# Modulation weights as raw stationary tiles with two columns moving, and value tiles behind the first scores

## Chip, cores and metric

One core of one Trainium2 chip runs the whole program. The metric is the device time of one execution in microseconds, from a few runs of the same kernel; beside them stands one profiled execution, on which all rows are.

## What is computed

A chain of transformer layers on 256 tokens of 1024 features, all float32. The first block has two layers with modulation: each takes a vector c (and c_ctx for the 256 context tokens) to six vectors of 1024 numbers, which scale, shift and gate its norms and its outputs. Layer 0 mixes with a differential attention and a neighbourhood attention over tokens and context, layer 1 with a grouped-query attention with sinks; each is followed by a SwiGLU network. The second block has four layers: sliding-window attention (swa), a gated linear recurrence, a latent attention (mla) and swa again, each followed by an attention over a memory of 256 tokens and by a convolutional feed-forward network. Cut to what the change touches:

```
for layer in range(2):
    mod_x = split(silu(c) @ ada_w[layer] + ada_b[layer], 6)          # ada_w: 1024 x 6144
    mod_c = split(silu(c_ctx) @ ada_w[layer] + ada_b[layer], 6)
    h_x = rmsnorm(x, g) * (1 + mod_x[1]) + mod_x[0]
    x = x + mod_x[2] * mixer(h_x, h_c)
    h_x = rmsnorm(x, g2) * (1 + mod_x[4]) + mod_x[3]
    x = x + mod_x[5] * swiglu(h_x)
```

## The kernel before

All weights come as one stream of 785 units of 128 x 1024 float32 (0.52 MB), in the order of use, into a ring of six slots (`RING`). SyncE's queue loads unit u once `unit_used` says that unit u - 6 is done (`load`, L532). A float32 product is made of three products of rounded halves: ScalarE copies a unit to `ring_high` (rounded, `feed`, L1205), GpSimd, or VectorE for the first 19 units (`early_low`, L2089), writes the rest in place as `ring_low` (`low_part`, L2393), and TensorE (PE) does high x high, high x low, low x high (`product`). The semaphores `unit_high` and `unit_ready` count the units in order; PE waits on those counts. Where nothing is rounded (scores, transposes, probabilities times values, sums by a product with `mean_of`) PE does full float32 products from the raw tiles.

The modulation weights are 96 units: 16 at the start (`ada0a`), 48 during the attention of layer 0 (`ada0b`; 8 groups of layer 0 and 4 of layer 1), 32 during that of layer 1 (`ada1`). Four units make a group of 512 modulations. `ada_products` (L689) moves the 512 columns of a weight row through PE against `cond4`, which holds the two condition vectors, each as high and low part, in its first columns: two k by two halves, four instructions a unit. The sums stand in 4 rows of a bank; ScalarE copies them to `ada_rows` (L1247), PE turns them in four small transposes (`ada_turn`, L707), ScalarE copies those to `ada_cols` (L1251), and VectorE adds the two parts and the bias into `mods` (`modulations`, L2066).

The start: PE does groups 0 to 3 and, between them, the squares of x (`squares_by_token`, L716: 8 tiles by 4 products, a 128x128 tile of squares stationary and one column of `mean_of` moving). Then `spread_both` (L727) spreads the norm's scale over a bank, VectorE scales x (`scaled_both`, L1811; after its first two instructions it does the rest of the gains and the last early low parts), and the first projection begins, `project("ab", ...)`.

Each attention is written for all engines with the same loop over steps (PE L843, ScalarE L1317, VectorE L1882): scores of later heads, row minima on VectorE, exponentials on ScalarE, transposes of the probabilities on PE, copies out of the bank, products with the values, a last transpose. Layer 0's (`at0`, 16 steps) and layer 1's (`at1`, 8 steps) go one step ahead and have modulation work in slots between their parts (`fill`, L855; the slots are written out in `ADA0` and `ADA1`, L2424); the others go two steps ahead. Their first scores wait for all queries, keys and values. The engines of a queue work in program order, so what is issued first is done first.

```
                    for e in part:
                        wait_unit(u + e)
                        for kk in range(2):
                            k = 2 * e + kk
                            w = unit(u + e, 512 * kk, 512)
                            c4 = cond4[:, 4 * k:4 * k + P]
                            one = pe.matmul(banks[b][:, :], c4, w[0], start=(k == 0), stop=False)
                            mm = pe.matmul(banks[b][:, :], c4, w[1], start=False, stop=(k == KD - 1))
                            release(one)
                        state["owed"] += 1
```

Of the kernel before, what the change touches and what calls it, by code (L numbers as in the profile page):

```python
# [8 lines left out]
P = 128  # L9
T = 256  # L10
# [12 lines left out]
N_COND = P + 4 * (KD - 1)  # L23
# [99 lines left out]
UNITS, N_UNITS = unit_bases()  # L123
COLS, N_COLS = column_layout()
# [30 lines left out]
def write_program(nc, ins, out, ledger):  # L155
# [7 lines left out]
    with ExitStack() as ctx:  # L163
# [23 lines left out]
        cond4 = sb("cond4", N_COND, fp32r)  # L187
        ada_rows = sb("ada_rows", 512)
        ada_cols = sb("ada_cols", 16)
# [335 lines left out]
        with nc.Block() as block:  # L525
# [3 lines left out]
            def _(sp):  # L529
# [51 lines left out]
            def _(pe):  # L581
# [8 lines left out]
                def wait_unit(u):  # L590
                    pe.wait_ge(unit_ready, u + 1)
# [13 lines left out]
                def wait_high(u):  # L605
                    pe.wait_ge(unit_high, u + 1)
# [11 lines left out]
                def project(st, u0, n_tiles, src, n, depth=KD, ready=None, base=0, per_unit=1, after=None):  # L618

                    width = P * per_unit  # L620
                    opened = 0
# [18 lines left out]
                    for m in range(opened, n_tiles):  # L640
# [3 lines left out]
                        b = m % 4  # L644
# [18 lines left out]
                def project_v(st, u0, n_groups, src, tok_tiles, depth=KD, width=T, units=2, after=None):  # L663


                    n = 0
                    per = depth // units
                    for j in range(n_groups):
                        u = u0 + units * j
                        for e in range(units):  # L670
                            wait_unit(u + e)
                        for t in range(tok_tiles):
                            b = n % 4
# [9 lines left out]
                            n += 1  # L683
                        state["owed"] += units
# [4 lines left out]
                def ada_products(l, g, u, part=range(4), b=7):  # L689

                    if 0 in part:
                        claim(b)
                    for e in part:
                        wait_unit(u + e)
                        for kk in range(2):
                            k = 2 * e + kk
                            w = unit(u + e, 512 * kk, 512)
                            c4 = cond4[:, 4 * k:4 * k + P]
                            one = pe.matmul(banks[b][:, :], c4, w[0], start=(k == 0), stop=False)
                            mm = pe.matmul(banks[b][:, :], c4, w[1], start=False, stop=(k == KD - 1))  # L700
                            release(one)
                        state["owed"] += 1
                    if 3 in part:
                        mm.then_inc(*mark(proj_ready, "ada", l, g))
                        reader[b] = ("ada_rows", l, g)

                def ada_turn(l, g, b=7):  # L707

                    pe.wait_ge(*when("ada_rows", l, g))
                    for t in range(4):  # L710
                        mm = pe.transpose(banks[b][:, 4 * t:4 * t + 4], ada_rows[0:4, P * t:P * (t + 1)],
                                          const("ident", P)[0:4, 0:4])
                    mm.then_inc(*mark(proj_ready, "ada_cols", l, g))
                    reader[b] = ("ada_colsread", l, g)

                def squares_by_token(st, part):  # L716

                    for k in part:
                        pe.wait_ge(*when(st, "sq", k))
                        for i in range(4):  # L720
                            mm = pe.matmul(banks[6][:, i:i + 1], sq2(k)[:, P * i:P * (i + 1)], mean_of[:, 0:1],  # L721
                                           start=(k == 0 and i == 0), stop=(k == KD - 1), skip_group_check=True)
                        if k == KD - 1:
# [119 lines left out]
                def attention(st, items, needs, ada=None):  # L843
# [11 lines left out]
                    def fill(slot):  # L855
                        if ada_fill(ada, slot):
# [3 lines left out]
                            else:  # L860
                                ada_turn(*group)

                    def scores(s, a):
# [6 lines left out]
                        if s == 0 and a == 0:  # L870
                            for ev in needs:
# [26 lines left out]
                    def values(s):  # L898
# [3 lines left out]
                        claim(b)  # L902
                        for n, (a, blocks) in enumerate(fulls(d)):
# [62 lines left out]
                def ffn(name, src, ready, aside=None):  # L966
# [13 lines left out]
                    def gate_up(r, t, halves=(0, 1)):  # L980
# [4 lines left out]
                        for half in halves:  # L985
                            u = gate_unit(t) + half
                            out = banks[4 + t % 2][:, T * half:T * (half + 1)]
                            pe.wait_ge(unit_high, r * (3 * BODY) + (u + 1))
# [1597 lines left out]
```

## Time and profile before

| | |
|---|---|
| median of 3 runs | 2815.99 us (2813.96 to 2816.88) |
| the profiled execution: its time | 2817.64 us |
| its span, first to last instruction | 2815.8 us |
| mean granted TensorE clock | 0.961 |
| PE busy | 2646.3 us (94%), 19840 instructions |
| GpSimd busy | 1819.9 us (65%) |
| ScalarE busy | 1465.3 us (52%) |
| VectorE busy | 1122.9 us (40%) |
| read from HBM | 418.52 MB, 149 GB/s over the span |

The granted clock is the share of full speed that the chip gave TensorE in a stretch; 1.00 is 2.4 GHz, 0.50 is 1.2 GHz. A matmul's busy time is longer than its distance from the next one, since they are pipelined: a price is best taken from the distance of starts. In the windows "x" counts instructions, and one float32 product in the code can be more than one. Two ways to name a line are used: that of the code, and that of a helper which several stages share (L601 to L616 are all projections, L879 all scores, L893 all transposes of probabilities, L908 all products with values).

### The profile page before, as it was taken

The page shows a single profiled execution, that of the slowest core. Times are in us where ns is not written, and L with a number is a line of the kernel's source. Part 1 is how long each engine was busy: PE and PEld are TensorE (multiplying, and loading weights), DVE is VectorE, ACT ScalarE, POOL GpSimd, SP SyncE. Part 2 cuts the span into 40 slices and gives each one's busy share as a digit, 9 for nine tenths or more (in the row PEclk, how much of TensorE's full clock was granted, in tenths as well). Part 3 has the DMA queues.
Part 4 walks back from the last instruction along what each step waited for, and adds up shares of the span by engine and source line. Part 5 has one row for each costly group of instructions (what it writes and reads, how often), then busy time and mean ns, then how long its engine had stood idle before and what let it go on. Part 6 is the DMA issues. An engine that isn't in the chain of part 4 may idle for free.

```text
span 2815.8 us, 52622 instructions
## 1 busy us (share of the span) xinstructions
PE 2646.3 (94%) x19840; PEld 2506.8 (89%) x19840; DVE 1122.9 (40%) x2642; ACT 1465.3 (52%) x2586; POOL 1819.9 (65%) x770
## 2 busy tenths in 40 slices
PE   7998889999999999999999998999989999989998
PEld 6887769999997899988899988899978899888998
DVE  5227634122155521234343365433443433463434
ACT  5326735445445544444555576555545555464655
POOL 0437647888875778772568865488645688535786
PEclk7999999999999999999999988999999999989999
DMA  6325424555543545541345543255423455323554
GB/s 226 120 82 173 149 91 166 184 180 180 185 158 126 190 160 182 179 146 65 120 157 179 183 134 130 100 188 185 149 91 120 139 182 182 125 76 113 172 180 141
DMA packets 115637, 421.75 MB, mean 150 GB/s; under 512 B 12832, under 2 KB 14112, under 8 KB 114976
## 3 DMA queue, kind: packets, MB, share of 16 engines
q1 hardware_dynamic: 115200, 417.00, 44.0%
q8 instruction: 111, 1.82, 0.3%
q10 hardware_dynamic: 288, 2.62, 0.3%
q14 instruction: 38, 0.31, 0.0%
HBM read 418.52 MB, written 1.05 MB: 149 GB/s over the span
## 4 chain that ended last, share of the span: by engine, by line
PE 50%; issue 22%; POOL 20%; DVE 4%; ACT 2%; DMA 1%; POOLq 0%; SPq 0%; DVEq 0%; ACTq 0%
POOL ring_low L2395 20%; PE bank L610 9%; PE bank L616 9%; PE bank L611 9%; PE bank L601 6%; PE bank L602 6%; PE bank L603 6%; PE bank L908 2%; PE bank L879 2%; PE bank L760 1%; ACT scr L1332 1%; PE bank L926 1%; PE bank L721 0%; PE bank L893 0%; DVE xt L2267 0%
## 5 line engine op out<-in xcount | busy, mean ns | idle before, releaser
L2395 POOL TENSOR_TENSOR ring_low<-ring,ring_high 128x1024 fp32r<-128x1024 f32 x766 | 1819.7, 2406 | 978.0 <-ACT ring_high L1210 767.3
L610 PE MATMUL bank<-high,ring_high 128*128 128x256 f32 (+1 forms) x3372 | 856.4, 290 | 3.6 <-ACT ring_high L1210 1.7
L611 PE MATMUL bank<-low,ring_high 128*128 128x256 f32 (+1 forms) x3372 | 849.5, 288 | 0.0
L610 PEld LDWEIGHTS bank<-high,ring_high 128*128 128x128 f32 x3372 | 647.1, 192 | 10.8 <-ACT ring_high L1210 4.3
L611 PEld LDWEIGHTS bank<-low,ring_high 128*128 128x128 f32 x3372 | 647.3, 192 | 6.4
L1440 ACT ACTIVATE ring_high<-ring 128x1024 fp32r<-128x1024 f32 x448 | 467.5, 1053 | 92.2 <-DMA ring<-in_units 91.7
L616 PE MATMUL bank<-high,ring_low 128*128 128x256 f32 (+1 forms) x3372 | 491.6, 288 | 0.0
L616 PEld LDWEIGHTS bank<-high,ring_low 128*128 128x128 f32 x3372 | 445.2, 192 | 5.6
L1210 ACT ACTIVATE ring_high<-ring 128x1024 fp32r<-128x1024 f32 x337 | 350.8, 1053 | 101.8 <-DMA ring<-in_units 100.8
L601 PE MATMUL bank<-hid_high,ring_high 128*128 128x256 f32 x1232 | 349.4, 284 | 10.2 <-DVE hid_low L2052 8.1
L602 PE MATMUL bank<-hid_low,ring_high 128*128 128x256 f32 x1232 | 348.6, 283 | 0.0
L603 PE MATMUL bank<-hid_high,ring_low 128*128 128x256 f32 x1232 | 348.6, 283 | 0.0
L2039 DVE SCALAR_TENSOR_TENSOR qt<-bank,cols,qt 128x255 f32<-128x255 f32 (+1 forms) x352 | 145.5, 475 | 420.6 <-ACT qt L1452 420.6
L601 PE MATMUL bank<-high,ring_high 128*128 128x256 f32 (+1 forms) x680 | 221.4, 326 | 44.0 <-DVE low L1776 19.4
L601 PEld LDWEIGHTS bank<-hid_high,ring_high 128*128 128x128 f32 x1232 | 236.4, 192 | 11.8 <-issue 8.3
L602 PEld LDWEIGHTS bank<-hid_low,ring_high 128*128 128x128 f32 x1232 | 236.5, 192 | 0.0
L603 PEld LDWEIGHTS bank<-hid_high,ring_low 128*128 128x128 f32 x1232 | 236.5, 192 | 0.0
L1452 ACT ACTIVATE qt<-bank,cols 128x256 f32<-128x256 f32 x176 | 89.7, 560 | 262.0 <-PE bank L616 259.8
L602 PE MATMUL bank<-low,ring_high 128*128 128x256 f32 (+1 forms) x680 | 215.6, 317 | 0.0
L603 PE MATMUL bank<-high,ring_low 128*128 128x256 f32 (+1 forms) x680 | 215.1, 316 | 0.0
L601 PEld LDWEIGHTS bank<-high,ring_high 128*128 128x128 f32 x680 | 147.5, 217 | 54.7 <-DVE low L1776 23.9
L1332 ACT ACTIVATE scr<-bank,soft 128x128 f32<-128x128 f32 (+2 forms) x208 | 105.8, 517 | 120.9 <-DVE soft L1915 75.1
(226 smaller groups left out, 3391.0 us busy)
## 6 DMA issues: line engine op xcount, KB each, us to landing
ring<-in_units SPq DMA_DIRECT2D x785, 512.0 KB, 3.3
xt<-in_x SPq DMA_DIRECT2D x2, 1024.0 KB, 7.2
nbias<-in_bias ACTq DMA_DIRECT2D x1, 1536.0 KB, 6.9
vt<-in_mem ACTq DMA_DIRECT2D x1, 1024.0 KB, 7.0
out_x<-xt SPq DMA_DIRECT2D x8, 128.0 KB, 1.7
consts<-in_consts SPq DMA_DIRECT2D x1, 832.0 KB, 8.8
cols<-in_cols SPq DMA_DIRECT2D x1, 639.0 KB, 5.6
consts<-in_consts SPq DMA_DIRECT2D x1, 512.0 KB, 6.3
```

The source lines that it names most:

```text
L601: first = pe.matmul(out, w[0], x[0], start=start, stop=False, **more)
L602: pe.matmul(out, w[0], x[1], start=False, stop=False, **more)
L603: return first, pe.matmul(out, w[1], x[0], start=False, stop=stop, **more)
L610: first = pe.matmul(out, w[0], x[0], start=start, stop=False)
L611: pe.matmul(out, w[0], x[1], start=False, stop=False)
L616: return pe.matmul(out, w[1], x[0], start=False, stop=stop)
L1210: act.activation(whole(ring_high, v), whole(ring, v), ACT.Copy).then_inc(unit_high, 1)
L1332: act.activation(probs(s, a, i, d, shallow), banks[b][:, at:at + d["nk"][i]], ACT.Exp, bias=one(NB, s, a, i), scale=-1.0, accum_out=one(SM ...
L1440: act.activation(whole(ring_high, u), whole(ring, u), ACT.Copy).then_inc(unit_high, 1)
L1452: act.activation(conv_buf(n, half), b[:, T * half:T * (half + 1)], ACT.Identity, scale=cols[:, bass.ds(r * BODY + w, 1)], bias=cols[:, bas ...
L2039: dve.scalar_tensor_tensor(out=dst[:, lag:T], in0=b[:, T * half:T * half + T - lag], scalar=cols[:, bass.ds(r * BODY + w, 1)], in1=dst[:, ...
L2395: pool.tensor_tensor(whole(ring_low, u), whole(ring, u), whole(ring_high, u).bitcast(fp32), ALU.subtract).then_inc(unit_ready, 1)
```

## The change

First, the 96 modulation units are no longer split. `WHOLE` lists them; `feed`, `early_low` and `low_parts` leave them out, and `split_units(u)` turns a unit's number into the count of split units up to it, for all waits on `unit_high` and `unit_ready`. `ada_products` waits for the unit's load alone, holds a 128x128 piece of the raw unit stationary and moves two columns of `cond`: 2 k by 4 pieces, eight products a unit, into 8 columns of a bank with features on partitions. `cond4`, `ada_rows`, `ada_cols`, `ada_turn` and both ScalarE copies go, and `modulations` is one VectorE addition from the bank. The start is reordered: x's first half is loaded ahead of units 6 and 7, the squares stand between groups 1, 2 and 3, the spread stands after the first unit of group 3, and `scaled_both` does half of its tiles before the rest of the gains. In the attentions VectorE does a group's `modulations` at the head of a step instead of its end.

Second, in each attention but the recurrence's layer the last value tiles (two; in mla all four; in the memory attentions the last two query tiles) are projected behind the first scores (`behind`), into other banks, and only the first product with values waits for them (`values_need`). `needs` is now asked at each step, so that a step's scores wait for its own queries.

```diff
                 load_consts(CONSTS["swap"], CONSTS["swa"], ident_loaded)
-                for u in range(3, 8):
+                for u in range(3, 6):
                     load(u)
                 load_x(0)
-                load(8)
-                load(9)
+                for u in range(6, 10):
+                    load(u)
                 load_x(1)
...
                 def ada_products(l, g, u, part=range(4), b=7):
                     if 0 in part:
                         claim(b)
                     for e in part:
-                        wait_unit(u + e)
+                        v = u + e
+                        pe.wait_ge(loaded[v % RING], 16 * (v // RING + 1))
                         for kk in range(2):
                             k = 2 * e + kk
-                            w = unit(u + e, 512 * kk, 512)
-                            c4 = cond4[:, 4 * k:4 * k + P]
-                            one = pe.matmul(banks[b][:, :], c4, w[0], start=(k == 0), stop=False)
-                            mm = pe.matmul(banks[b][:, :], c4, w[1], start=False, stop=(k == KD - 1))
-                            release(one)
+                            for m in range(4):
+                                w = whole(ring, v)[:, 512 * kk + P * m:512 * kk + P * (m + 1)]
+                                mm = pe.matmul(banks[b][:, 2 * m:2 * m + 2], w, cond[:, 2 * k:2 * k + 2],
+                                               start=(k == 0 and m == 0), stop=(k == KD - 1), skip_group_check=True)
+                                release(mm)
                         state["owed"] += 1
...
                     for s in range(ahead):
                         for a in range(2):
                             scores(s, a)
+                    if behind:
+                        behind()
                     for s in range(last + 1):
...
-                ada_turn(0, 0, ADA_BANK[0])
-                first_ada(1, [1, 2, 3])
-                first_ada(2, [0])
-                ada_turn(0, 1, ADA_BANK[1])
-                first_ada(2, [1])
+                first_ada(1)
                 squares_by_token("n0", range(4))
-                first_ada(2, [2, 3])
+                first_ada(2)
                 squares_by_token("n0", range(4, KD))
                 first_ada(3, [0])
-                ada_turn(0, 2, ADA_BANK[2])
+                pe.wait_ge(ident_loaded, 16)
+                spread_both("n0")
                 first_ada(3, [1, 2, 3])
-                spread_both("n0")
-                ada_turn(0, 3, ADA_BANK[3])
...
-                project_v("ab", UNITS["ab"] + 16, 4, tokens(0, 2 * T), 4)
-                attention("at0", steps_at0(), ab_needs, ada=ADA0)
+                values_ab(range(0, 14))
+                attention("at0", steps_at0(), lambda s: ab_needs if s == 0 else [], ada=ADA0,
+                          behind=lambda: values_ab(range(14, 16), bank=lambda n: n - 8), values_need=[("ab", "vout", 15)])
...
-                        project_v(st + "v", u + 10, 1, tokens(0), 2)
-                        rotate(st + "q", 7)
+                        def needs(s, st=st):
+                            return [(st + "q", "rope", s), (st + "k", "rope", 1)]
+                        def behind(st=st, u=u):
+                            rotate(st + "q", 7)
+                            project_v(st + "v", u + 10, 1, tokens(0), 2, bank=lambda n: 6 + n)
...
                     while fed[0] < min(u + ahead, N_UNITS):
                         v = fed[0]
-                        act.wait_ge(loaded[v % RING], 16 * (v // RING + 1))
-                        act.activation(whole(ring_high, v), whole(ring, v), ACT.Copy).then_inc(unit_high, 1)
+                        if not is_whole(v):
+                            act.wait_ge(loaded[v % RING], 16 * (v // RING + 1))
+                            act.activation(whole(ring_high, v), whole(ring, v), ACT.Copy).then_inc(unit_high, 1)
                         fed[0] += 1
...
-                def modulations(l, g):
-                    dve.wait_ge(*when("ada_colsread", l, g))
-                    parts = ada_cols[:, :].rearrange("p (m e s) -> p m e s", e=2, s=2)
-                    link(dve.tensor_tensor(sm(88, 0, 8).rearrange("p (m s) -> p m s", s=2), parts[:, :, 0, :],
-                                           parts[:, :, 1, :], ALU.add))
+                def modulations(l, g, b=7):
+                    dve.wait_ge(*when("ada", l, g))
-                    dve.tensor_tensor(dst, sm(88, 0, 8).rearrange("p (m s) -> p m s", s=2),
+                    dve.tensor_tensor(dst, banks[b][:, 0:8].rearrange("p (m s) -> p m s", s=2),
                                       bias.unsqueeze(2).to_broadcast([P, 4, 2]), ALU.add
                                       ).then_inc(*mark(dve_done, "mods", l, g))
...
-                for u in range(EARLY, 4 * RING):
-                    low_part(0, u)
...
+                low_parts(EARLY, UNITS["ada0b"])
+                low_parts(UNITS["ab_out"], UNITS["ada1"])
+                low_parts(UNITS["c_out"], N_UNITS)
```

## Rows read from the trace of the kernel before

**Rows 1.** The page: busy us by engine, GB/s in 40 slices, the chain that ended last.

```profile
PE 2646.3 (94%) x19840; PEld 2506.8 (89%) x19840; DVE 1122.9 (40%) x2642; ACT 1465.3 (52%) x2586; POOL 1819.9 (65%) x770
...
GB/s 226 120 82 173 149 91 166 184 180 180 185 158 126 190 160 182 179 146 65 120 157 179 183 134 130 100 188 185 149 91 120 139 182 182 125 76 113 172 180 141
...
PE 50%; issue 22%; POOL 20%; DVE 4%; ACT 2%; DMA 1%; POOLq 0%; SPq 0%; DVEq 0%; ACTq 0%
```

**Rows 2.** Groups by line: out<-in, shapes, count | busy us, mean ns | idle before, releaser.

```profile
L2395 POOL TENSOR_TENSOR ring_low<-ring,ring_high 128x1024 fp32r<-128x1024 f32 x766 | 1819.7, 2406 | 978.0 <-ACT ring_high L1210 767.3 <-ACT ring_high L1440 209.7
...
L699 PE MATMUL bank<-ring_high,cond 128*128 128x512 f32 x192 | 88.5, 461 | 17.4 <-DVE ring_low L2093 12.0 <-ACT ada_cols L1256 5.3
...
L721 PE MATMUL bank<-mean_of,scr 128*128 128x1 f32 x64 | 13.6, 347 | 0.0
...
L711 PE MATMUL bank<-consts,ada_rows 4*128 4x4 f32 x96 | 10.3, 209 | 5.6 <-ACT ada_rows L1249 5.6
```

**Rows 3.** Timeline of PE, start: start us, us, line, count, [idle before <-releaser].

```profile
7.54 0.77 PE L699 MATMUL bank<-ring_high,cond 128*128 128x512 f32 x1 [7.54 <-DVE ring_low L2093]
...
22.87 0.80 PE L699 MATMUL bank<-ring_high,cond 128*128 128x512 f32 x1 [3.92 <-DVE ring_low L2093]
...
57.07 0.80 PE L601 MATMUL bank<-high,ring_high 128*128 128x512 f32 x1 [5.17 <-DVE low L1824]
```

**Rows 4.** Timeline of ScalarE, 4 to 6 us; ring<-in_units is unit 0.

```profile
5.08 1.06 ACT L1210 ACTIVATE ring_high<-ring 128x1024 fp32r<-128x1024 f32 x1 [0.60 <-DMA ring<-in_units]
```

**Rows 5.** Windows, one-column products alone: us, busy (x), granted clock, DMA share, GB/s.

```profile
27.27:33.95 6.68, 6.68 (x32) 0.50 0.25 83
37.51:44.19 6.68, 6.68 (x32) 0.50 0.28 78
2408.53:2411.12 2.59, 2.59 (x24) 1.00 0.10 41
```

**Rows 6.** Windows, all of PE, the same columns.

```profile
202.80:206.00 3.20, 3.20 (x8) 0.50 0.00 0
206.30:366.50 160.20, 140.42 (x946) 1.00 0.48 161
1298.50:1308.50 10.00, 10.00 (x50) 0.50 0.35 107
2411.20:2414.70 3.50, 3.48 (x17) 0.50 0.00 0
```

**Rows 7.** Timeline of PE, at0's first step and its end.

```profile
201.26 1.30 PE L893 MATMUL bank<-consts,scr 128*128 128x128 f32 x8 [1.65 <-ACT scr L1332]
...
206.05 0.52 PE L699 MATMUL bank<-ring_high,cond 128*128 128x512 f32 x1
...
207.10 0.60 PE L893 MATMUL bank<-consts,scr 128*128 128x128 f32 x4
...
368.13 0.80 PE L601 MATMUL bank<-high,ring_high 128*128 128x512 f32 x1
```

**Rows 8.** PE's waits in at0, 195 to 371 us: us, times, longest.

```profile
PE bank L908 <- DVE scr L1925: 5.5, 3, 2.0
PE bank L699 <- ACT ada_cols L1256: 5.0, 7, 1.8
PE bank L711 <- ACT ada_rows L1249: 4.7, 4, 2.5
```

**Rows 9.** Timeline of PE where attentions begin (968.84: at1's end).

```profile
867.93 1.75 PE L893 MATMUL bank<-consts,scr 128*128 128x128 f32 x8 [2.55 <-ACT scr L1332]
...
968.84 0.38 PE L601 MATMUL bank<-high,ring_high 128*128 128x256 f32 x1
...
1291.69 1.66 PE L879 MATMUL bank<-kt,qt 64*128 64x128 f32 x16 [0.96 <-DVE qt L1702]
...
1294.54 0.52 PE L893 MATMUL bank<-consts,scr 128*128 128x128 f32 x3 [1.19 <-ACT scr L1332]
...
1383.90 1.35 PE L879 MATMUL bank<-xt,qt 128*128 128x256 f32 x5 [0.47 <-ACT qt L1219]
```

More of the change, by code:

```diff
@@ L22 @@
 PEELED = range(2 + BODY * LOOPS, FT)
-N_COND = P + 4 * (KD - 1)
 EPS_RMS = 1e-6
@@ L123, with is_whole, split_units @@
 UNITS, N_UNITS = unit_bases()
+WHOLE = [range(UNITS[name], UNITS[name] + size) for name, size in (("ada0a", 16), ("ada0b", 48), ("ada1", 32))]
+def is_whole(u):
+    return any(u in part for part in WHOLE)
+def split_units(u):
+    return sum(not is_whole(v) for v in range(u + 1))
 COLS, N_COLS = column_layout()
@@ L669, in project_v @@
                         u = u0 + units * j
-                        for e in range(units):
-                            wait_unit(u + e)
                         for t in range(tok_tiles):
-                            b = n % 4
+                            n += 1
+                            if part and n not in part:
+                                continue
+                            if t == 0 or part and n == part[0]:
+                                for e in range(units):
+                                    wait_unit(u + e)
+                            b = bank(n)
                             claim(b)
@@ L704, in ada_products @@
                         mm.then_inc(*mark(proj_ready, "ada", l, g))
[L705 to L714, printed above, removed]
+                        reader[b] = ("mods", l, g)
                 def squares_by_token(st, part):
@@ L841, in stats_summed, with attention @@
                     return after
-                def attention(st, items, needs, ada=None):
+                def attention(st, items, needs, ada=None, behind=None, values_need=()):
                     shallow = ada is not None
@@ L869, in scores @@
                         h = d["heads"][a]
-                        if s == 0 and a == 0:
-                            for ev in needs:
+                        if a == 0:
+                            for ev in needs(s):
                                 pe.wait_ge(*when(*ev))
@@ L902, in values @@
                         claim(b)
+                        for ev in values_need if s == 0 else ():
+                            pe.wait_ge(*when(*ev))
                         for n, (a, blocks) in enumerate(fulls(d)):
@@ L1298, in shifted, with shifted_both @@
                                        ).then_inc(*mark(act_done, st, "high", k))
-                def shifted_both(st, l, part):
-                    for k in range(KD):
+                def shifted_both(st, l, part, tiles=range(KD)):
+                    for k in tiles:
                         for s in range(2):
@@ L1315, in affine, with attention @@
                                        ).then_inc(*mark(act_done, st, "value", k))
-                def attention(st, items, ada=None, late=None):
+                def attention(st, items, ada=None, late=None, behind=None):
                     shallow = ada is not None
@@ L1880, in residual_ffn, with attention @@
                                                                *([] if k == KD - 1 else [k])))
-                def attention(st, items, ada=None):
+                def attention(st, items, ada=None, behind=None):
                     shallow = ada is not None
@@ L1988, in attention @@
                             lowest(s, a)
+                    if behind:
+                        behind()
                     for s in range(last + 1):
+                        if ada_fill(ada, 5 * s):
+                            modulations(*ada_fill(ada, 5 * s)[0])
                         out_pt(s, 0)
@@ L2187, in _, with values_ab @@
                 rope_group(ROT0[4:8])
-                evacuate_v("ab", 16, lambda n: V(n % 4, 256 * (n // 4), 256 * (n // 4) + 256))
-                attention("at0", steps_at0(), ada=ADA0)
+                def values_ab(part, **more):
+                    evacuate_v("ab", part, lambda n: V(n % 4, 256 * (n // 4), 256 * (n // 4) + 256), **more)
+                values_ab(range(0, 14))
+                attention("at0", steps_at0(), ada=ADA0, behind=lambda: values_ab(range(14, 16), bank=lambda n: n - 8))
                 gains_of(0, 1)
```

236 lines of the change are left out of this document (102 added, 134 removed).

## Prediction

> **What bounds the kernel now.** The page first: TensorE is busy 94% of the span, and PE and its "issue" time make most of the chain that ended last. GpSimd's 20% there lies in stretches where PE hardly waits [rows 1]. So I ask first what an edit puts on PE, and only then what it takes from others. The groups by line give the modulation work: 192 products with the high part (as many with the low part), 512 columns moving, 96 small transposes, and 64 instructions of the squares, which already have the new form: a raw 128x128 stationary tile and one column moving [rows 2]. Those 64 are 32 products in the code (8 tiles by 4), so a full float32 product is two instructions on PE, while a product of rounded halves is one.
>
> The timeline of the start shows what ends there: the first projection begins at 57.07. PE first works at 7.54, waits 3.92 us for VectorE's low parts, and from 22.87 works almost without a gap [rows 3]. Unit 0's bytes are there at 5.08 [rows 4].
>
> Then the granted clock, which decides this case. In the two runs of squares PE is busy without a gap and stays at 0.50, the 1.2 GHz level, though 3.6 us of 512-column modulation products lie between them [rows 5]. At 2408.53 PE comes at 1.00 (2.4 GHz) from dense 256-column work and does one-column products without a gap; after 2.6 us of them it stands at 0.50 [rows 5, 6]. The first swa attention, all products of 64 to 128 columns, ran 10 us at 0.50 with PE busy throughout. Against that, at0 held 1.00 from 206.3 to 366.5, but a good part of its work is the 512-column modulation products, which the change removes. And from 202.8 to 206 the engine did 512-column score products at 0.50 and was at 1.00 right after [rows 6].
>
> **The change part by part.** Reference is the profiled execution, 2817.64 us, 1.65 above the median of the runs shown.
>
> *A unit on PE.* Before: four instructions of 512 columns, 206.05 to 207.10, 1.05 us [rows 7]. After: 8 products, 16 instructions. At 2.4 GHz 24 one-column instructions took 2.59 us, 0.108 each [rows 5]: 1.73 us a unit, with a little for the change of shape 1.78, which is 0.73 more. At 1.2 GHz 32 took 6.68, 0.209 each [rows 5]: 3.34 us a unit. The second column adds one element; I take nothing for it. From below, the bound is one instruction a product, 0.87 us; the count of the squares excludes it. From above, the 0.209 of the lower clock is the bound. The Trainium skill says in "FP8 and Floating Point Precision", TensorE Precision Notes, that true FP32 takes four passes through the array; if each pass were an instruction with a load of its own, a unit would be 3.46 us and the sum with the attentions at full clock 3033 instead of 2845. The trace has two instructions a product, so I keep 1.78.
>
> *The start.* 16 units no longer wait for ScalarE's copy or VectorE's low part. PE can begin at 5.1, when unit 0 has landed; cond is ready before. PE then takes 16 x 3.34 = 53.5, the squares 64 x 0.209 = 13.4, the spread's four transposes 4 x 0.209 = 0.8: 5.1 + 67.7 = 72.8, against 57.07: **+15.8**. I take 1.2 GHz throughout because no 512-column product is left in this stretch. The bounds: at 2.4 GHz PE would be through at about 41, and the tiles scaled on VectorE and unit 18's low part would hold the projection until about 44, -13. SP's queue has x's first half ahead of units 6 and 7; that costs nothing, since 0.52 MB in PE's 3.34 us of a unit is 157 GB/s, and the first slice moved 226 [rows 1]. The squares' new releases and the four lines of gains moved on VectorE are under PE's work too, which is the cover; without it they would cost about a microsecond.
>
> *at0*, 48 units. From its first transposes at 201.26 to the next projection at 368.13 are 166.9 us [rows 7]. At 2.4 GHz: 48 x 0.73 = +35.0; 12 groups of four small transposes, 10.3/24 = 0.4 each, -4.8 [rows 2]; PE's waits for the two ScalarE copies of a group, 5.0 + 4.7, all go [rows 8]; with 48 high parts and the copies off ScalarE and 48 low parts, 115 us, off GpSimd, I take another 2.8 of its waits: 184.6, **+17.7**.
>
> *at1*, 32 units. 867.93 to 968.84 is 100.9 us [rows 9]. +23.4 for the units, -3.2 for the transposes, -0.5 for their waits: 120.6, **+19.7**.
>
> *The clock in both.* After the change a step of at1 is 1.9 us of 512-column scores, then some 12 us of 64- and 128-column products with four unbroken 1.78 us stretches of two-column ones. The nearest rows are the run at 2408 and the first swa attention, both at 0.50 while busy; the score products may bring the clock back, as at 202.8 [rows 5, 6]. I choose two thirds of the time at 1.2 GHz, at which time is 1.5 times the work. Taking 7 and 4 us of waits out of the work: at0 (184.6 - 7) x 1.5 = 266, +99.5; at1 (120.6 - 4) x 1.5 = 175, +74.0. Ends: none of the time (+17.7, +19.7) and all of it (+188, +132).
>
> *Late value tiles and query tiles.* Two tiles of dense products now stand behind the first scores, where PE waits for ScalarE's first exponentials: 1.65 in at0 [rows 7], 2.55 in at1, 0.96, 1.19 and two more at the first swa attention and like ones at the second, 0.47 and one more at each of four memory attentions, about 1 in mla: some 16 us [rows 9]. Both swa attentions ran some ten us at 0.50 just behind those waits [rows 6]; with the clock kept VectorE limits a step, so I take a third of it, 8. Together **-24**; ends 0 and -30. VectorE copies the late tiles behind its first minima and PE claims banks 4 to 7, free by then; in swa the last rotation waits behind the scores and only step 7 needs it. Nothing queued behind is short of time.
>
> *GpSimd and ScalarE.* 80 low parts go from GpSimd (193 us of its 1820) [rows 2] and 96 copies from ScalarE; neither ends a wait in the projections that follow, so nothing beyond the above. In the FFNs nothing changes.
>
> *Sum:* 15.8 + 99.5 + 74.0 - 24 = +165.3; 2817.6 + 165.3 = 2982.9; less 1.65 for the median, **2981 us**. A difference of 0.2%, 5.6 us, is about what a measurement of this kernel can tell from no change.
>
> **The rivals.**
>
> *R1, the clock holds in the attentions.* at0 kept 1.00 through stretches with PE partly idle, 140 us busy of 160 [rows 6], and the dense scores come every step. Then 15.8 + 17.7 + 19.7 - 24 = +29.2: 2845. Chance 0.17.
>
> *R2, faster: ScalarE, VectorE and GpSimd relieved, at full clock.* Its place is the start and the waits inside at0 and at1; it decides only if two-column products hold 2.4 GHz. The start gives -13; with the expected waits that is -13 + 17.7 + 19.7 - 24 = +0.4: 2816, no change. If the relief also takes the rest of PE's waits there, whose largest is 5.5 us in at0 [rows 8], some 15 in at0 and at1 together, 2801. Against it: the one-column runs. Chances 0.04 for 2816, 0.05 for 2801. The Trainium skill leans this way: "TensorE: Matmul & The Clock Gate", Why this matters for your kernels, asks only that the engine be kept busy without idle gaps, and the new products leave none. By that rule the start and both attentions would be at 2.4 GHz and the time 2816. The trace disagrees near 2408: PE without a gap, and the clock at 0.50 after it.
>
> *R3, the late tiles move the wait instead of removing it:* the first transposes, now behind two tiles of products, find a wait for the probabilities or the value copies as long as before. 2981 + 24 = 3005. The waits are shorter than the tiles that go in, which speaks against. Chance 0.08.
>
> *R4, 1.2 GHz for all of both attentions:* 15.8 + 188 + 132 - 24 = +312: 3128. The dense scores speak against. Chance 0.06.
>
> *Does it do what it says?* Yes: the units are raw, the copies and low parts gone. The question is only the price.
>
> **How the numbers follow.** The forecast has 0.60, and covers 2920 to 3030 as the share of the attentions' time at 1.2 GHz goes from 0.45 to 0.8, and some 20 us more on either side for the other terms' ends. The range reaches down to R1 and up past R3, 2841 to 3050; outside are R2, R4 and the forecast's tail. Faster 0.06 (R2's lower form and the edge of the other), the same 0.03, slower 0.91.
>
> **What would show it.** Right: the ada line with 16 instructions a unit and 1536 in all, starts 0.108 or 0.209 apart; the first projection near 73 at a clock of 0.50 from 5 us on; 0.50 over much of at0 and at1, with returns to 1.00 after score products; no wait longer than 0.5 us ahead of the first transposes; stages outside the attentions unmoved. Wrong: a first projection before 57 (the start's clock), 1.00 throughout at0 (R1), or a unit in 8 instructions. If PE waits long in at0 for something other than the ada lines, my relief of ScalarE was misjudged.

## The result, and the profile after

The changed kernel takes **2992.77 us** (median of 5 runs, 2981.05 to 3041.55) against 2816.88 us (2813.96 to 2822.78) for the kernel before: a ratio of 1.0606, with a 95% interval from 1.0575 to 1.0637. The forecast was 2981, inside 2841 to 3050. Ratios, here and below, leave out the executions over 1.5% above the fastest of their kernel (here 3028.01 and 3041.55 us); medians take in all of them.

The profiled execution is the longest of the five. The mean granted clocks of the five, in order of time, are 0.925, 0.921, 0.921, 0.909 and 0.905: from the fastest to the slowest the time at 0.50 grows by some 130 us (an estimate: twice the lost share of each span), and work at 0.50 takes twice its time, which makes 65 us, near the 60.5 between them. So the five differ by their time at the lower clock, and sizes are taken from the profiled one with care and checked on other runs.

The page after (busy us by engine, granted clock in 40 slices, the chain that ended last), to be read against [rows 1]:

```profile
PE 2915.9 (96%) x20896; PEld 2792.1 (92%) x20896; DVE 1057.0 (35%) x2599; ACT 1358.8 (45%) x2442; POOL 1632.0 (54%) x690
...
PEclk9996556999999755999989999999999999999998
...
PE 44%; issue 36%; POOL 16%; DVE 2%; ACT 1%; DMA 0%; POOLq 0%; SPq 0%; ACTq 0%; DVEq 0%
```

ScalarE, VectorE and GpSimd are all less busy than before, by 107, 66 and 188 us. TensorE is 270 us busier. The clock row has two dents down to 5 tenths (6556 and 755): the two attentions that carry modulation units. The groups by line, for [rows 2]:

```profile
L2384 POOL TENSOR_TENSOR ring_low<-ring,ring_high 128x1024 fp32r<-128x1024 f32 x686 | 1631.8, 2411 | 1387.8 <-ACT ring_high L1237 1178.9
...
L715 PE MATMUL bank<-cond_silu,ring 128*128 128x2 f32 x1536 | 292.4, 322 | 5.4 <-DMA ring<-in_units 5.4
```

1536 instructions for 96 units: 16 a unit, two for each of its 8 products. 80 low parts have left GpSimd. The start on TensorE, for [rows 3, 4]:

```profile
5.41 27.44 PE L715 MATMUL bank<-cond_silu,ring 128*128 128x2 f32 x128 [5.41 <-DMA ring<-in_units]
32.71 6.97 PE L728 MATMUL bank<-mean_of,scr 128*128 128x1 f32 x32
39.54 13.79 PE L715 MATMUL bank<-cond_silu,ring 128*128 128x2 f32 x64
53.19 6.97 PE L728 MATMUL bank<-mean_of,scr 128*128 128x1 f32 x32
...
74.42 0.77 PE L609 MATMUL bank<-high,ring_high 128*128 128x512 f32 x1
```

27.44 us for 128 instructions is 0.214 each, the pace of the 0.50 level in [rows 5]. This trace's first record of the clock comes at 80 us; ahead of that the clock row shows 9 for want of a record, and the pace has to tell the clock. The first projection starts at 74.42, without a gap ahead of it, 17.35 us later than before. The windows of the two attentions (all of TensorE: us, busy, granted clock, DMA share, GB/s), and a piece of the first's timeline:

```profile
208.53:513.74 305.21, 302.39 (x1553) 0.60 0.27 86
1002.27:1201.12 198.85, 196.76 (x1025) 0.62 0.26 88
224.00:244.00 20.00, 20.00 (x85) 0.50 0.25 86
288.70:350.00 61.30, 61.30 (x276) 0.50 0.26 86
```

```profile
217.87 1.99 PE L886 MATMUL bank<-kt,qt 64*128 64x512 f32 x8
219.79 1.95 PE L715 MATMUL bank<-cond_silu,ring 128*128 128x2 f32 x16
221.60 1.07 PE L900 MATMUL bank<-consts,scr 128*128 128x128 f32 x8
...
290.59 3.76 PE L917 MATMUL bank<-vt,scr 128*128 128x128 f32 x16
294.14 3.41 PE L715 MATMUL bank<-cond_silu,ring 128*128 128x2 f32 x16
297.41 3.76 PE L917 MATMUL bank<-vt,scr 128*128 128x128 f32 x16
```

A unit runs from 219.79 to 221.60, 1.81 us, while the clock is up, and from 294.14 to 297.41, 3.27 us, in the stretch at 0.50. The engine has no gap in either; it is busy for all 61.3 us of the long stretch. The other products pay too: 16 instructions of value products take from 290.59 to 294.14 there, 3.55 us, where one_of_16 at full clock has 1.79 (below). From the first transposes to the next projection at0 takes 296.85 us (166.87 before), 245.6 of them at 0.50; at1 takes 191.07 (100.91), 151.4 of them at 0.50. Start +17.4, at0 +130.0 and at1 +90.2 are 237.5 us; the two profiled executions differ by 223.9, so all other places together give back 14.

The clock goes up and down within a step. A piece of at1, by windows and by timeline (scores of 512 columns at L886, then a unit, then transposes):

```profile
1083.90:1107.80 23.90, 23.78 (x102) 0.50 0.20 69
1107.90:1111.10 3.20, 2.85 (x26) 1.00 0.51 164
```

```profile
1103.30 3.79 PE L886 MATMUL bank<-kt,qt 64*128 64x512 f32 x8
1107.03 2.30 PE L715 MATMUL bank<-cond_silu,ring 128*128 128x2 f32 x16
1109.18 1.07 PE L900 MATMUL bank<-consts,scr 128*128 128x128 f32 x8
```

In both attentions together the clock falls 15 times, each time shortly behind a unit of two-column products, and rises 13 times, 12 of them during or just behind score products (256 or 512 columns) and once behind products with values.

### The profile page after: what moved, and what is told of

Its sections match the earlier page's. It is cut to its first block, busy times and chain, and to the rows that moved or that the text cites. A ratio compares the mean times of both kernels' runs of the same rounds, so it can differ in the third digit from the quotient of the medians.

```text
span 3039.5 us, 54371 instructions
## 1 busy us (share of the span) xinstructions
PE 2915.9 (96%) x20896; PEld 2792.1 (92%) x20896; DVE 1057.0 (35%) x2599; ACT 1358.8 (45%) x2442; POOL 1632.0 (54%) x690
## 3 DMA queue, kind: packets, MB, share of 16 engines
HBM read 418.52 MB, written 1.05 MB: 138 GB/s over the span
## 4 chain that ended last, share of the span: by engine, by line
PE 44%; issue 36%; POOL 16%; DVE 2%; ACT 1%; DMA 0%; POOLq 0%; SPq 0%; ACTq 0%; DVEq 0%
POOL ring_low L2384 16%; PE bank L618 8%; PE bank L619 8%; PE bank L624 8%; PE bank L609 5%; PE bank L610 5%; PE bank L611 5%; PE bank L715 2%; PE bank L886 1%; PE bank L917 1%; PE bank L769 1%; DMA ring<-in_units 0%; PE bank L728 0%; PE bank L935 0%; DVE scr L1760 0%
## 5 line engine op out<-in xcount | busy, mean ns | idle before, releaser
L2384 POOL TENSOR_TENSOR ring_low<-ring,ring_high 128x1024 fp32r<-128x1024 f32 x686 | 1631.8, 2411 | 1387.8 <-ACT ring_high L1237 1178.9
L618 PEld LDWEIGHTS bank<-high,ring_high 128*128 128x128 f32 x3372 | 647.2, 192 | 10.6 <-ACT ring_high L1237 3.5
L1451 ACT ACTIVATE ring_high<-ring 128x1024 fp32r<-128x1024 f32 x448 | 466.2, 1054 | 76.6 <-DMA ring<-in_units 76.4
L715 PEld LDWEIGHTS bank<-cond_silu,ring 128*128 128x128 f32 x1536 | 293.2, 294 | 25.0 <-issue 23.9
L1237 ACT ACTIVATE ring_high<-ring 128x1024 fp32r<-128x1024 f32 x241 | 251.8, 1053 | 108.7 <-DMA ring<-in_units 108.1
L715 PE MATMUL bank<-cond_silu,ring 128*128 128x2 f32 x1536 | 292.4, 322 | 5.4 <-DMA ring<-in_units 5.4
```

The costliest lines, as they stand in the source:

```text
L618: first = pe.matmul(out, w[0], x[0], start=start, stop=False)
L715: mm = pe.matmul(banks[b][:, 2 * m:2 * m + 2], w, cond[:, 2 * k:2 * k + 2], start=(k == 0 and m == 0), stop=(k == KD - 1), skip_group_chec ...
L1237: act.activation(whole(ring_high, v), whole(ring, v), ACT.Copy).then_inc(unit_high, 1)
L1451: act.activation(whole(ring_high, u), whole(ring, u), ACT.Copy).then_inc(unit_high, 1)
L2384: pool.tensor_tensor(whole(ring_low, u), whole(ring, u), whole(ring_high, u).bitcast(fp32), ALU.subtract).then_inc(unit_ready, 1)
```

## The experiments

### The two parts alone

*late_only* is the kernel before with the late value and query tiles only. *raw_only* is the kernel after with those tiles put back where they were. What each edit does in the first attention:

```diff
 # late_only, against before
-project_v("ab", UNITS["ab"] + 16, 4, tokens(0, 2 * T), 4)
+values_ab(range(0, 14))
+attention("at0", ..., behind=lambda: values_ab(range(14, 16), bank=lambda n: n - 8), values_need=[("ab", "vout", 15)])
 # raw_only, against after
-values_ab(range(0, 14))
+project_v("ab", UNITS["ab"] + 16, 4, tokens(0, 2 * T), 4)
...
```

> Only the late value tiles; the modulation units stay split, cast and turned as before. The forecast priced this part at -24 us (16 us of waits for value tiles and query rotation ahead of the first transposes, 8 us of clock at the three sliding-window attentions), with ends 0 and -30: about 2793 us, inside 2787 to 2817. The rival, in which the moved tiles only shift the wait to a later place, expects 2817 us or slightly more. In the trace of the whole change the places of this part add up to about -14 us, which would be 2803 us.

> Only the raw units: full float32 products with two columns moving, value tiles where they were. The forecast's terms without the late tiles are +15.8 (start), +99.5 (first attention) and +74.0 (second), +189 us: 3006 us. By the stages of the trace of the whole change the raw part costs more, +17 +130 +90 or about +237 us in that long execution, and about +190 us in an execution at the median. If the two parts were not additive (the late tiles giving the half clock a better or worse hour), the sum of this run's and the late run's differences would miss the +176 us of the whole change by more than 5 us.

Measured: late_only 2798.83 us, ratio 0.9932 (0.9904 to 0.9961), against 2817.66 for the kernel before beside it: -19, by the interval -11 to -27. That excludes a wait that is only moved (2817), and neither the forecast's -24 nor the -14 of the trace. raw_only 3021.41 us, ratio 1.0689 (1.0643 to 1.0736): +194 by the ratio, +204 by the medians, a little more than the forecast's +189. Together +6.89% and -0.68%, +6.2%, where the whole change has +6.06%: by the ratios the parts add up, within their intervals. By the medians they miss the +176 by 9 us, more than the 5 us of the expectation, but raw_only's own executions are 53 us apart.

Where the tiles act can be read from TensorE's idle time around the first transposes. From 3 us ahead of the first scores to 6 us behind the first transposes, in all nine attentions together, it is 16.7 us in the kernel before and 1.5 us in late_only, so the waits that the forecast put at some 16 us are gone. A part comes back elsewhere. The waits of TensorE over the whole span, in the kernel before and then in late_only (us in total, times, longest):

```profile
PE bank L893 <- ACT scr L1332: 7.9, 8, 2.5
...
PE bank L926 <- ACT scr L1345: 2.8, 5, 1.0
```

```profile
PE bank L934 <- ACT scr L1378: 7.4, 9, 1.9
```

The first transposes' waits for the probabilities, 7.9 us, are gone (late_only has no such line among its longest seventeen). The output's transposes (L926, now L934) wait 4.6 us longer for ScalarE. That looks like rival R3 in part; that it is the same wait, moved, is not shown. The clock term of the sliding-window attentions, 8 us, is not a steady gain: late_only's first such attention has 17.1 us at 0.50 (10.2 before), its second none (13.7 before). The waits account for some 11 of the 19 us; where the rest lies, within so wide an interval, is open.

raw_only's attentions, all of TensorE:

```profile
214.91:479.17 264.26, 259.28 (x1505) 0.68 0.29 99
973.12:1167.85 194.73, 190.09 (x976) 0.62 0.27 90
```

From first transposes to the next projection these are 260.6 and 190.2 us. at1 is within a microsecond of the long execution of the whole change; at0, at 167.1 us of half clock, is 36 us shorter than there. This suggests that the whole change's executions differ mostly by how long at0 stays down, but only one of them was profiled, so it is not shown. raw_only's four runs spread from 2997.59 to 3050.65.

### Is it the columns?

*wide128* and *wide64* are the kernel after; only the moving operand and the output of a product are wider, and the modulations are read out of every 128th or 64th column:

```diff
-mm = pe.matmul(banks[b][:, 2 * m:2 * m + 2], w, cond[:, 2 * k:2 * k + 2], ...)
+mm = pe.matmul(banks[b][:, n * m:n * m + n], w, cond[:, 2 * k:2 * k + n], ...)   # n = 128 or 64
```

> The whole change, but each product of the modulations moves 128 columns instead of 2 (the 126 beyond are zeros or the next features' columns, and are not read). Same number of products, same order, same units. My theory: the half clock belongs to TensorE working with two columns in each product, and not to the raw units, the order or the waits. Then the granted clock is back at 1.00 in both attentions (half clock in them under 20 us in all, after 397 us), at0 takes 185 to 190 us from its scores to the next projection (296.9 with two columns), at1 121 to 125 us (191.1), the first projection starts before 60 us, and the time is 2790 to 2850 us. The rival that full float32 products lower the clock whatever they move expects about 2990 us, and one that each product pays by its columns expects the clock back but a unit of 3.5 us and more instead of 1.78: 2870 us or more.

> The same with 64 columns moving. If the columns moved in a stretch decide the clock, this lies between 128 columns (2790 to 2850 us by my theory) and 2 columns (2990 us), nearer to the first if 64 is still enough for long stretches at 1.00. If only the kind of product counts, it is 2990 us as with two columns. At full clock a product with 64 columns should cost the same 0.108 us as one with 2, if the duration of such a product is an issue time and not a time by columns.

Measured: wide128 **2815.75 us**, ratio 0.9988 (0.9962 to 1.0015), four runs from 2812.97 to 2819.19. 126 more columns, of zeros and neighbours, in every product take some 177 us off. wide64 2842.63 us, ratio 1.0084 (1.0058 to 1.0111). The windows of both attentions, of wide128 and then of wide64:

```profile
180.30:371.75 191.45, 187.88 (x1553) 1.00 0.41 136
858.19:986.16 127.97, 125.54 (x1025) 1.00 0.41 136
```

```profile
208.10:398.43 190.33, 186.75 (x1553) 1.00 0.41 137
885.18:1012.41 127.23, 124.80 (x1025) 1.00 0.41 137
```

The same 1553 and 1025 instructions as in the whole change, and no time at 0.50. From first transposes to the next projection: 183.08 and 120.20 us with 128 columns, 181.97 and 119.45 with 64. (The expectation mixed two measures: its 296.9 and 191.1 count from the first transposes, though it says from the scores. From there the two attentions take 191.45 and 127.97 us, somewhat above its ranges; from the transposes they are somewhat below.) The starts, of wide128 and of wide64:

```profile
5.40 16.04 PE L716 MATMUL bank<-cond_silu,ring 128*128 128x128 f32 x128 [5.40 <-DMA ring<-in_units]
21.28 3.63 PE L729 MATMUL bank<-mean_of,scr 128*128 128x1 f32 x32
...
47.97 0.48 PE L609 MATMUL bank<-high,ring_high 128*128 128x512 f32 x1
```

```profile
5.33 27.54 PE L716 MATMUL bank<-cond_silu,ring 128*128 128x64 f32 x128 [5.33 <-DMA ring<-in_units]
32.67 6.93 PE L729 MATMUL bank<-mean_of,scr 128*128 128x1 f32 x32
```

With 128 columns the clock comes up in the start; with 64 it does not (0.215 an instruction, and no record of the clock before 79.5 us), and the first projection begins at 74.34 instead of 47.97. Those 26 us are nearly the whole difference of the two runs, 27 us. In the attentions, among score products and others, the clock stays up in both runs. So the lower clock in the attentions comes with the two columns of these products; full float32 as such, the raw units and the order of the work are excluded as its cause, since wide128 has all three. The columns moved and the columns written to the bank grew together in these runs, and which of them counts was not told apart. (The 0.108 us of the expectation is the time of one of a product's two instructions: a unit of 16 takes 1.79 us in wide128's at0.)

### What a unit costs when the clock holds

*one_of_16* is wide128 with one product a unit left in the attentions; the other products of those modulations are left out, so it computes other modulations (`b == 7` is an attention):

```diff
-for m in range(4):
+for m in range(4) if b != 7 else [e] if kk else []:
 ...
```

> The change with 128 columns moving, and in the two attentions only one product of each unit's 16 (so 15 of 16 products of those modulations are left out; the units are still loaded and released). It prices a raw unit: if its 15 products are pure TensorE time of 0.108 us each, at0 shortens by 48 times 1.62 or 78 us, from 183.1 to about 105, and at1 by 32 times 1.62 or 52 us, from 120.2 to about 68. If other waits (softmax on ScalarE and VectorE, or the units' transfers) stand behind the products, the attentions shorten by less: with those bounds nearer to 130 and 85 us the extra products would have been half hidden.

The expectation miscounted: a unit has 8 products and 16 instructions, so 7 products, 14 instructions, are left out, and at 0.108 each that predicts 73 us less in at0 and 48 in at1. Measured, from first transposes to the next projection: 109.95 and 74.66 us, 73.1 and 45.5 less. (One run, 2704.48 us.) Its timeline, with the two instructions that are left of a unit:

```profile
195.06 0.39 PE L716 MATMUL bank<-cond_silu,ring 128*128 128x128 f32 x2
195.28 1.95 PE L918 MATMUL bank<-vt,scr 128*128 128x128 f32 x16
```

In at0 73.1/48/14 is 0.109 us for an instruction, all of it on the path; in at1 0.102, so 3 us of 48 were hidden. TensorE is the bound of these attentions, and at full clock a unit costs what its instructions take.

### One-column products elsewhere, and a version that is faster

*before_wide* is the kernel before with its one-column products widened to 128. *mixed* has raw units with 128 columns for the start alone, the split, cast units of the kernel before in the attentions, and the late tiles. *mixed_wide* is mixed and *wide_all* is wide128 with the wide sums:

```diff
 # before_wide, mixed_wide, wide_all
-mm = pe.matmul(banks[6][:, at + i:at + i + 1], x[:, P * i:P * (i + 1)], mean_of[:, 0:1], ...)
+mm = pe.matmul(banks[6][:, P * (at + i):P * (at + i + 1)], x[:, P * i:P * (i + 1)], mean_of[:, :], ...)
 # and the same in squares_by_token
 # mixed, mixed_wide, against wide128 (b == 7 is an attention)
+if b == 7:
+    wait_unit(v)
 ...
+    c4 = cond4[:, 4 * k:4 * k + P]
+    one = pe.matmul(banks[b][:, :], c4, w[0], start=(k == 0), stop=False)
+    mm = pe.matmul(banks[b][:, :], c4, w[1], start=False, stop=(k == KD - 1))
 ...
```

> The kernel before, with its own one-column products widened to 128 columns: the squares of the start and the sums of every layer norm (the same number of products, four regions of a bank instead of four columns). If few columns a product also cause the half clock that the kernel before had (231 us in all: some at the start, and 7 to 10 us at each layer norm and 19 us at the last), it drops below 120 us, the first projection starts about 7 us sooner (before 57.1 us), and the time is 2760 to 2795 us. If the clock at the norms falls because TensorE waits there, only the start gains: 2808 to 2817 us, with 180 us or more left at half clock.

> The parts that pay, together: raw units in the start alone, with 128 columns moving; in the two attentions the split, cast units of the kernel before; the late value tiles; and the one-column sums of the norms widened to 128 columns. By the stages of the traces so far: start -9 us (first projection 48.0 instead of 57.1), attentions as before (165 and 101 us), late tiles -19 us, and by the norms' clock 0 to -40 us: 2790 us with no gain at the norms, 2750 us with all of it. If it is not below the run of the late tiles alone (2799 us), the start's gain is given back later.

> The whole change with 128 columns moving in the modulations (2816 us), and the one-column sums widened too. The same gain at the norms as in the widened kernel before, whatever it is, and none or a few us at the start, whose first projection already starts at 48.0 us: 2770 to 2812 us. Against the mixed version it should be slower by the price of raw units in the attentions, 35 us (16 to 18 us at the first and 19 us at the second).

> The mixed version (raw units with 128 columns at the start, split units in the attentions, late value tiles) with the one-column sums left at one column. The mixed version with wide sums gave 2775 us where the stages without a gain at the norms had promised 2790 us. If the wide sums give the difference, this run is at 2786 to 2794 us, and its half clock in all is 50 us or more above the 134 us of the wide one. If it is at 2775 to 2780 us, the sums gave nothing, as their -4 us in the kernel before may mean, and the start gives more than its own 9 us.

| kernel | us | ratio to before (95%) | first projection | us at 0.50 in all |
| --- | --- | --- | --- | --- |
| before_wide | 2812.66 | 0.9979 (0.9956 to 1.0001) | 48.60 | 187 |
| wide_all | 2807.04 | 0.9957 (0.9933 to 0.9980) | 45.56 | 145 |
| mixed | 2788.36 | 0.9889 (0.9862 to 0.9917) | 44.87 | 201 |
| mixed_wide | **2775.44** | 0.9842 (0.9805 to 0.9879) | 45.06 | 134 |

The last column counts the stretch ahead of a trace's first clock record (8 to 12 us; 80 in the whole change) as 0.50. By it the kernel before has 231 us, wide128 172, the whole change 663. In before_wide the start is 8.5 us shorter, as both theories said. At eight of the norms the stretch at 0.50, 7 or 10 us long, shrinks to half or less; 187 us remain in all, above the line drawn for the columns and near the one for waiting. Both seem to play a part: those eight stretches shrink with the wide sums, and behind the last norm of the kernel before the clock is down with hardly an instruction running (the same columns):

```profile
2803.70:2815.00 11.30, 0.67 (x3) 0.50 0.27 93
```

before_wide also had 24 us at 0.50 in the attention of the second block's third layer (mla), which none of its edits touches, on products that ran at full clock in the kernel before:

```profile
2066.91:2106.57 39.66, 37.69 (x152) 0.70 0.04 14
2069.40:2093.30 23.90, 23.90 (x66) 0.50 0.06 22
```

That took 11 us (12.99 + 26.67 from its first scores to its end, instead of 8.32 + 20.58), and in the profiled execution hides most of what the norms gave. mixed against mixed_wide gives the wide sums 0.5%, wide128 against wide_all 0.3%; the intervals of each pair overlap, so a gain of 0.2 to 0.5% is likely, not established. mixed fell where the expectation had the case in which the sums are what differs, and has 67 us more at 0.50. But 6.5 of the 13 us between them lie in the first sliding-window attention (first scores to next projection), at 0.50 for 17.1 us in mixed and not at all in mixed_wide; wide_all, with the wide sums, stands there as mixed does:

```profile
1266.00:1310.34 44.34, 40.10 (x275) 0.81 0.11 36
```

```profile
1268.91:1306.72 37.81, 32.44 (x275) 1.00 0.12 43
```

```profile
1300.38:1344.72 44.34, 40.10 (x276) 0.81 0.11 37
```

mixed_wide beats both kernels. Its page:

```profile
PE 2623.1 (95%) x20016; PEld 2497.7 (90%) x20016; DVE 1106.3 (40%) x2623; ACT 1446.9 (52%) x2562; POOL 1823.9 (66%) x770
...
PEclk9999999999999999999999998999999999999999
```

Against the kernel before it is 1.6%, 44 us by the ratio, faster: 12 from the start (first projection 45.1 instead of 57.1), about 19 from the late tiles, and some 13 from the clock, at the norms and in that attention. Of the 12 us at the start before_wide, which still has split units there, gets 8.5 by its wide sums alone; what the raw units add to that is 3 to 4 us (48.60 against 45.06). Against wide_all, -32: in the attentions the split units of 1.05 us are cheaper than raw ones of 1.8 (168.9 and 100.4 us instead of 183.1 and 120.2).

## Why the prediction was right, point by point

**What bounds.** Right. TensorE was the bound of the start and both attentions, and 188 us off GpSimd and 107 off ScalarE bought no more than the waits that they ended (below).

**A unit on PE, 1.78 us at 2.4 GHz and 3.34 at 1.2.** Right: 1.81 and 3.27. The bound of one instruction a product, 0.87 us, is excluded by the count of 1536. The page "FP8 and Floating Point Precision" of the Trainium skill, TensorE Precision Notes, was weighed for a unit of 3.46; the trace has two instructions a product, and the unit at full clock takes 1.81.

**The start, +15.8.** Measured +17.35: 72.8 forecast, 74.42 there. The 1.6 us are nearly all in the pace, 0.213 to 0.214 an instruction instead of 0.209. The other bound, -13 at full clock, is near what mixed shows: 44.87, -12.2.

**at0 and at1 at full clock, 184.6 and 120.6 us.** wide128 ran them at full clock in 183.08 and 120.20. The units' price, the transposes and the relieved waits were well sized. The waits went almost entirely. TensorE's waits in wide128's at0 are 3.6 us in all, where the three lines of [rows 8] have 15.2:

```profile
PE bank L947 <- DVE scr L1916: 1.9, 4, 0.6
PE bank L936 <- DVE scr L1916: 1.0, 3, 0.3
PE bank L936 <- DVE scr L1955: 0.7, 1, 0.7
```

**The share of time at 1.2 GHz, two thirds in both.** The mechanism was right: two-column products brought the clock down and score products brought it back. The size was a choice between far ends. at1, from first transposes to the next projection: 78% of the time is at 0.50 in raw_only and 79% in the whole change, and 190.2 and 191.1 us came instead of 175. So the at1 term, +74.0, is the one that was mis-sized; it measured +89 to +90. at0: 64% and 260.6 us in raw_only, 83% and 296.9 in the profiled run of the whole change, against 266. With at1's 16 us, 2 at the start and 5 at the late tiles, the sum would miss by more than the 12 us between 2981 and 2993; what is left for at0 in an execution at the median is some +88 instead of +99.5, an estimate by subtraction, on terms of which the late tiles alone are uncertain by 8 us. raw_only measured +93.8. That the total came within 12 us is in part luck: the errors have both signs, and the executions themselves are 60 us apart.

**Late tiles, -24.** Measured -19 (-11 to -27), which does not exclude -24. The waits around the first transposes went as said, 16.7 us down to 1.5; 4.6 us of waits appeared at the outputs' transposes, and the clock term of 8 us, a third of the sum, was not a steady gain.

**The rivals.** R1 and R2 assumed that two-column products hold the clock. They do not; but wide128 is the world of R2, start gained and both attentions at 1.00, and its 2815.75 us is R2's 2816. In part that is chance: its start gives -9.1 for -13, the attentions +16.2 and +19.3, so all other places must give some 27, where R2 had 24 and the late tiles measured 19 by themselves. By the rule of the Trainium skill that R2 leaned on ("TensorE: Matmul & The Clock Gate", Why this matters for your kernels: keep the engine busy, without idle gaps) the change should have held 2.4 GHz. The trace disagrees: 61.30 us busy of 61.30, at 0.50. R3 was at most partly true: 4.6 us of waits turned up elsewhere, not 24. R4, 0.50 for all of both attentions, did not happen: the clock came back with the score products, as [rows 6] had shown at 206.

## What to carry to other kernels

At full clock a product with one or two columns moving took as long here as one with 128 (0.108 to 0.113 us for each of its two instructions). Where products of two columns made up about half of the work of an attention, TensorE was at half clock for 64 to 83% of it, and the wider products among them paid as well. So look at the granted clock in busy stretches before moving wide work into narrow products; and where narrow products cannot be avoided, widening their moving operand with columns that nobody reads is worth a run: here it gave back 177 of the 194 us that the raw units cost. Work taken off engines that do not bound a stage (188 us of GpSimd, 107 of ScalarE) is worth only the waits that it ends. That is why the cheaper split units won in the attentions, and raw ones only at the start, where the engine had waited for split ones; even there most of the gain was to be had by widening the sums.

## What the runs showed of the hardware that was not expected

Columns of zeros that nobody reads make a kernel faster: 2993 us with 2 columns, 2816 with 128, with the same count of instructions. At full clock 64 and 128 columns differ by 0.6% of at0's time (181.97 and 183.08 us).

The kernels with long stretches at the lower clock also scattered more. The whole change's executions spread over 2.0% (2981.05 to 3041.55, at mean clocks from 0.925 to 0.905) and raw_only's over 1.8%, wide128's over 0.2% (2812.97 to 2819.19, at 0.974 to 0.971). Why the share of time at the lower clock differs between executions of one kernel was not found.

In the same place the clock can go either way from one kernel to another that does not differ there: the third layer's attention stood at 0.50 for 23.9 us in before_wide and for none in the ten other traces of this study, that of the kernel before among them. What decides it there was not found.
